# Reading an expert's down weights in 8 KB runs, with the hidden layer turned by every fourth column

## What is computed

```python
D_MODEL, SEQ, N_EXPERTS, TOP_K = 1024, 256, 8, 2
D_FF_EXPERT = 7 * D_MODEL // 2            # 3584

def swiglu(x, w_gate, w_up, w_down):
    return (jax.nn.silu(x @ w_gate) * (x @ w_up)) @ w_down

def moe_swiglu(x, w_router, w_gate, w_up, w_down):
    logits = xt @ w_router
    top_val, top_idx = lax.top_k(logits, TOP_K)
    top_w = jax.nn.softmax(top_val, axis=-1)
    gates = jnp.sum(jax.nn.one_hot(top_idx, N_EXPERTS) * top_w[..., None], axis=1)
    for e in range(N_EXPERTS):
        y = y + gates[:, e:e + 1] * swiglu(xt, w_gate[e], w_up[e], w_down[e])
```

## Time and profile before

| what | value |
|---|---|
| median of 3 runs | 1483.78 us (1482.41 to 1484.92) |
| the profiled execution's own time | 1482.4 us |
| its span, first to last instruction | 1480.5 us |
| mean granted TensorE clock, as a share of full | 0.993 |
| busy share: PE, PEld, DVE, ACT, POOL | 97%, 83%, 75%, 65%, 7% |
| bytes read from memory | 428.5 MB |
| loads of expert weights | 336 of 1 MB, 112 of them down |

### The profile page before, as it was taken

How to read it: one execution, slowest core, us unless ns; L and a number is a source line. 1 busy time by engine, 2 the same in 40 slices (tenths; PEclk the granted TensorE clock), 3 DMA queues, 4 the chain that set the end, 5 groups by cost and what they waited for, 6 DMA issues and landing times.

```text
span 1480.5 us, 20902 instructions
## 1 busy us (share of the span) xinstructions
PE 1433.6 (97%) x7756; PEld 1225.7 (83%) x7756; DVE 1115.3 (75%) x829; ACT 957.3 (65%) x856; POOL 109.4 (7%) x91
## 2 busy tenths in 40 slices
PE   6989999999999989999999999999999999999996
PEld 5887899998988778888888888888888888888885
DVE  4474554446455578888888888889898889888886
ACT  5383434345354467777777777777777777777774
POOL 3141000000000110001001002002001000000100
PEclk9999999999999999999999999999999999999999
DMA  9513666554512489999999999999999999999993
GB/s 337 188 58 111 181 197 195 175 197 158 172 57 86 158 303 388 373 355 394 388 350 396 387 375 379 392 369 368 395 372 363 394 394 353 395 377 357 388 394 124
DMA packets 205946, 436.46 MB, mean 295 GB/s; under 512 B 8016, under 2 KB 53328, under 8 KB 205904
## 3 DMA queue, kind: packets, MB, share of 16 engines
q1 hardware_dynamic: 198160, 418.01, 77.6%
q0 software_dynamic: 3024, 11.01, 2.5%
q10 hardware_dynamic: 4720, 6.88, 1.7%
HBM read 428.54 MB, written 7.34 MB: 294 GB/s over the span
## 4 chain that ended last, share of the span: by engine, by line
PE 92%; DVE 4%; ACT 2%; issue 1%; DMA 1%; DVEq 0%; SPq 0%; ACTq 0%
PE banks L1197 29%; PE banks L1199 29%; PE banks L1198 28%; PE banks L1506 2%; PE banks L1355 1%; DVE w_lo L769 1%; DVE xn L782 1%; PE banks L1253 1%; DMA xres<-in_x 1%; ACT arena L556 0%; PE banks L1212 0%; PE banks L1474 0%; DVE arena L910 0%; ACT xn L456 0%; PE banks L1343 0%
## 5 line engine op out<-in xcount | busy, mean ns | idle before, releaser
L769 DVE TENSOR_TENSOR w_lo<-raw,w_hi 128x2048 fp32r<-128x2048 f32 x397 | 906.1, 2291 | 222.3 <-ACT w_hi L442 221.2
L442 ACT CAST w_hi<-raw 128x2048 fp32r<-128x2048 f32 x397 | 758.5, 1911 | 242.8 <-PE banks L1199 238.0
L1197 PE MATMUL banks<-w_hi,t_hi 128*128 128x512 f32 (+2 forms) x1088 | 416.3, 383 | 5.8 <-DVE w_lo L769 2.7
L1199 PE MATMUL banks<-w_lo,t_hi 128*128 128x512 f32 (+2 forms) x1088 | 410.6, 377 | 0.0
L1198 PE MATMUL banks<-w_hi,t_lo 128*128 128x512 f32 (+2 forms) x1088 | 410.3, 377 | 0.0
L1197 PEld LDWEIGHTS banks<-w_hi,t_hi 128*128 128x128 f32 x1088 | 205.3, 189 | 42.7 <-DVE w_lo L769 3.0
L1199 PEld LDWEIGHTS banks<-w_lo,t_hi 128*128 128x128 f32 x1088 | 205.0, 188 | 38.3
L1198 PEld LDWEIGHTS banks<-w_hi,t_lo 128*128 128x128 f32 x1088 | 205.4, 189 | 36.1 <-issue 0.2
L1197 PE MATMUL banks<-w_hi,h_hi 128*128 128x512 f32 x536 | 209.6, 391 | 0.7 <-DVE w_lo L769 0.7
L1199 PE MATMUL banks<-w_lo,h_hi 128*128 128x512 f32 x536 | 208.8, 389 | 0.0
L1198 PE MATMUL banks<-w_hi,h_lo 128*128 128x512 f32 x536 | 208.7, 389 | 0.0
(11 more groups left out here) (209 smaller groups left out, 907.2 us busy)
## 6 DMA issues: line engine op xcount, KB each, us to landing
raw<-in_moe_w_gate SPq DMA_DIRECT2D x112, 1024.0 KB, 7.4
raw<-in_moe_w_up SPq DMA_DIRECT2D x112, 1024.0 KB, 7.7
raw<-in_moe_w_down SPq DMA_DIRECT2D x112, 1024.0 KB, 7.6
raw<-in_na_w_qkv SPq DMA_DIRECT2D x12, 1024.0 KB, 5.1
raw<-in_ffn_w_gate SPq DMA_DIRECT2D x11, 1024.0 KB, 5.4
raw<-in_ffn_w_up SPq DMA_DIRECT2D x11, 1024.0 KB, 5.4
raw<-in_ffn_w_down SPq DMA_DIRECT2D x11, 1024.0 KB, 4.9
raw<-in_w_in_e SPq DMA_DIRECT2D x7, 1024.0 KB, 12.2
```

The lines of the kernel that those rows point to most:

```text
L442: act.copy(w_hi[:, u.part, 0:n], raw[:, u.raw, 0:n]).then_inc(hi_done, 1)
L769: dve.tensor_tensor(w_lo[:, u.part, 0:n], raw[:, u.raw, 0:n], w_hi[:, u.part, 0:n].bitcast(F32), ALU.subtract).then_inc(lo_done, 1)
L1197: pe.matmul(out, a_hi, b_hi, start=start, stop=False)
L1199: return pe.matmul(out, a_hi, b_lo, start=False, stop=stop)
```

## The change

The down weights are viewed so that weight row 512 j + 4 p + r of an expert goes to partition p as block r. A unit of two blocks is then one run of 8 KB for each partition, and runs of neighbouring partitions are 16 KB apart; the two units of a step take the two halves of each 16 KB. To match, block k of the turned hidden layer takes the columns k, k + 4, k + 8 and so on of `hid`, a step of 4 floats or 16 bytes, in place of 128 neighbouring columns.

```diff
-        w_ed = moe_w_down[0].rearrange("e (k p) n -> e p k n", p=P)
+
+        w_ed = moe_w_down[0].rearrange("e (j p r) n -> e j p r n", p=P, r=4)
...
             def down(e, j, base, c):
                 for i in range(2):
-                    load(unit_of(base, *c[i]), w_ed[e, :, bass.ds(j * 4 + 2 * i, 2), :])
+                    load(unit_of(base, *c[i]), w_ed[e, j, :, 2 * i:2 * i + 2, :])
...
                 for k in range(4):
-                    last = pe.transpose(banks[:, 6, k * P:(k + 1) * P], hid[:, k * P:(k + 1) * P], ident)
+                    last = pe.transpose(banks[:, 6, k * P:(k + 1) * P], hid[:, k:HALF:4], ident)
```

## The result

The changed kernel takes 1485.45 us in the median of 20 runs (1483.57 to 1488.67), the one before 1483.51 us in 20 runs beside it (1481.04 to 1485.49). The ratio is 1.0017 with a 95% interval of 1.0010 to 1.0024: slower by 0.1 to 0.24%. The forecast was no change at 1483.5 us.

The account below looks back on a forecast made before the run. PE was taken to set the pace, with the weight stream running at its demand. Load, contraction order and turn each added 0 to the profiled 1482.4 us; with the runs' median 1.4 above it, the forecast was 1483.5 us, range 1480.5 to 1504.

Parts of the forecast that it names:

- The load: Down-weight loads in the experts: longer runs gain 0 to 0.4 us, taken as 0, since landings have 4.7 us of cover.
- the stated band: Down loads in the profile after: landing expected in 7.1 to 7.7 us in the median.
- Rival B: Down loads get slower and the weight stream binds, from 15% dearer on; 1512 us at 25% dearer; chance 0.07.
- The turn: Four PE transposes in each of 56 turns, now reading `hid` with a step: 0 taken, up to 64 us.
- the load has 63 ns of room: Turn's weight load on PE: 44 ns of reading under the moving identity's 107 ns, so a slower read stays hidden.
- the half rate: Turn's weight load reading at half speed: 88 ns of reading, still hidden under the identity, cost 0.
- rival A: Second to fourth weight load of each turn on PE's chain gets dearer, kernel slower: 1495 to 1502 us; chance 0.21.
- a quarter of the rate: Turn's weight load at 176 ns of reading: three loads stick out by 69 ns, 11 us, or 14 with the first.
- two signs named for A: In the turn: four transposes taking 0.7 us and more, and their weight loads lasting over 200 ns instead of 138.
- a range of free rates: Turn's weight load: anything down to 0.83 ns a column, 2.4 times the present time, was held to cost nothing.
- The first load: Each turn's first weight load, under a 0.23 us matmul: more room; at 270 ns against 230 it adds 40 ns.
- The upper bound: Turn's weight loads at 427 ns each: three times 0.32 plus 0.20 us, 1.16 us a turn, 64 us in all.

Follow-up runs that it names:

- the turn alone: Kernel before, with the turn taking every fourth column of `hid` and the down loads still in two 4 KB rows: 1485.71 against 1482.83 us, ratio 1.0025.
- the load alone: Changed kernel with the old turn of 128 neighbouring columns, so only the down loads' 8 KB runs are new: ratio 1.0001 (0.9991 to 1.0010).

## Why the prediction was wrong, point by point

- **The bound.** Right. PE sets the pace and the stream runs at PE's demand: with the turn as before, 8 KB runs change the stage by 0.1 us, the reading's resolution.
- **The load, 0 (0 to 0.4 gained).** Right, and measured alone: ratio 1.0001. The packet counts came out to the packet, and the landing in the stated band. Rival B fell: ACT has no wait for a transfer left, and in the two stretches of the earlier trace rows the stream moved 398 GB/s where it had 394, and 358 where it had 355. Those stretches are no test of the limit any more, since no late landing stands ahead of the first.

```profile
1395.00:1440.00 45.00, 45.00 (x206) 37.40 (x205) 39.47 (x22) 33.07 (x21) 0.00 (x0) 1.00 1.04 398
612.00:662.00 50.00, 50.00 (x229) 41.58 (x228) 44.30 (x27) 39.03 (x28) 1.69 (x1) 1.00 1.00 358
```

- **The turn, "I take 0".** This is the term that failed; it measured 3.0 us (3.2 alone). The step of the reasoning that failed is "the load has 63 ns of room", with the half rate "still hidden": the load rose by 71 ns to 209. The place was the one that rival A names, the weight loads of the turn on PE's chain, and its dividing line, the identity's 0.83 ns a column, was drawn at about the right spot: with the load at 209 ns the pitch rises, with 168 and 187 it does not. But A was priced only at a quarter of the rate and beyond, 11 us and more, with nothing between that and 0, and the loss of 3 us fell into the gap. Of the two signs named for A, the load over 200 ns came and the four transposes at 0.7 us did not. I had entered a range of free rates as if it were a likelihood. That the time still came out 2 us from the forecast is the smallness of this loss, not the mechanism: the forecast said that the turn's pitch would not change.
- **The first load, taken as covered.** By the starts in the traces the first transpose comes 5 ns later than before. The upper bound is also summed wrongly here: by the way the quarter rate is worked out, a first load of 94 + 427 ns sticks out of 230 by 0.29 us and not 0.20, which makes 1.25 us a turn and 69 us in all in place of 64.
- **The reading of the load's length.** I split 138 ns into 44 of reading and 94 of latency from two contiguous loads. With 94 off, the 209 ns leave 115 of reading, 8 ns over the identity's 107, near the 12 ns by which the pitch grew. But with a step of 4, 128 and 96 columns take 209 and 168 ns, 1.28 ns a column, which leaves 45 as the fixed part, and by that the load would have stood out by 57 ns. So the split does not carry over, and a load's length in the list is not the time for which it blocks the next.
- **"Hidden is free".** 1.3 to 1.6 us remain where the pitch is unchanged (96 columns, steps of 8 and 16), and 23 of the 60 ns a step in the changed kernel lie outside the turn too. The prediction had no term for them. The traces place them: 5 to 9 ns a step ahead of the turn, 18 to 24 behind it (none there with a step of 2). Their cause stays open, as does what the load's length depends on.
- **The rule of 16-byte lines.** The Trainium skill, SBUF — State Buffer (Door 1: The DMA port swizzle), spoke against this edit, and the direction was right: every step but 1 made the load longer. Its condition was not borne out: with a step of 2, two accesses fall to each 16-byte line, which by that page is enough for full bandwidth, and the load took 207 ns and the moving side half its rate. The same passage counts 4 fp32 as a step that is free, which would have spoken for this edit; the load took 209 ns. The measurement decides: here every step that was tried in a PE operand costs.

## What to carry to other kernels

A layout that makes transfers longer bought nothing here, where the engine, not the stream, sets the pace. Before such a layout moves a cost, ask on which engine the permutation has to be undone, and put it on one with room (DVE here: 0.4 us a step more, and no loss), not into an operand of the engine on the chain. Where a price is unknown and the chain has no slack at all, work out the small prices as well as the large ones: 12 ns on three of four places in 55 turns, and what comes with them, are a measurable loss. For differences of a few us, compare the length of the stage that was changed within the traces rather than two spans.

## What the runs showed that was not expected

- A step in a TensorE operand has a price from 2 columns on: the transposing weight load 138 to 207 ns, the ordinary one, fp32r, 188 to 290 (step of 4), the moving fp32r operand from 0.23 to 0.45 us for 512 columns. In the load it is largest at 2 and 4 and lower at 8 and 16 (187, 186 ns).
- DVE's 128x512 product with a step of 4 columns on both inputs, or of 128 on the output, takes 1089 and 1101 ns in place of 681.
- Most of the spread between these profiled executions lies ahead of the experts. The stage was 935.1 to 935.3 us in the four profiled kernels whose matmuls are those of before, and 938.3 and 938.5 in the two with the new turn, while its first turn began anywhere from 520.6 to 523.9 us. The granted clock goes with it. Ahead of the first turn it stood at its lower level (1.2 of 2.4 GHz) for 6.8 us in all where that turn began at 520.6 and 520.7, for 10.2 us where it began at 521.8 and 522.1, and for 13.6 us where it began at 523.8 and 523.9. A stretch that shows it, in the turn alone and then in the load alone (us from start, us, busy times, clock, share, GB/s):

```profile
490.00:520.00 30.00, 27.16 (x158) 21.57 (x158) 14.06 (x41) 12.99 (x18) 5.93 (x13) 0.94 0.43 159
```

```profile
490.00:520.00 30.00, 28.00 (x149) 21.94 (x150) 13.89 (x39) 12.12 (x16) 5.89 (x13) 0.83 0.36 127
```
